# Loads of x and of the first weights asked for in turn, and x transposed and split inside the first product item of a two-block transformer kernel

## What is computed

```
def rmsnorm(x, g):
    xf = x.astype(jnp.float32)
    y = xf * lax.rsqrt(jnp.mean(xf * xf, axis=-1, keepdims=True) + EPS)
    return (y * g.astype(jnp.float32)).astype(x.dtype)
...
        h = rmsnorm(x, g_mix[l])
        z = jnp.einsum('bsd,dc->bsc', h, w_in[l])
        cb, cc, cv, q, k, v, f_logit, gate_c, gate_a = jnp.split(z, SPLIT_POINTS, axis=-1)
```

## Time and profile before

| what | us |
|---|---|
| time, median of 3 runs | 2446.07 |
| lowest and highest of them | 2444.16, 2447.24 |
| the profiled execution's own time | 2443.27 |
| its span in the trace | 2441.5 |

### The profile page before, as it was taken

One profiled execution on the slowest core, in us unless ns is written; L12 is line 12 of the kernel. 1 busy time (PEld: TensorE's weight loads), 2 busy tenths in 40 slices (PEclk: granted clock), 3 DMA queues, 4 the chain that ended last, 5 costly groups with the idle time before them and its releaser, 6 DMA issues.

```text
span 2441.5 us, 30339 instructions
## 1 busy us (share of the span) xinstructions
PE 2418.8 (99%) x12645; PEld 2060.3 (84%) x12645; DVE 1515.2 (62%) x1534; ACT 1168.7 (48%) x1360; POOL 0.2 (0%) x4
## 2 busy tenths in 40 slices
PE   8999999999999999999999999999999999999999
PEld 6788888888888888888888888888888888888887
DVE  5565566666566556566456666855777577756774
ACT  5444444545544344344344545554555455535552
POOL 0000000000000000000000000000000000000000
PEclk9999999999999999999999999999999999999999
DMA  7546556565555565655665555545656665566564
GB/s 227 175 151 192 158 183 188 183 189 189 189 178 189 195 216 184 195 177 198 195 185 177 198 153 172 172 170 179 189 175 206 190 189 174 200 195 181 183 203 143
DMA packets 236902, 450.58 MB, mean 185 GB/s; under 512 B 16449, under 2 KB 19643, under 8 KB 236635
## 3 DMA queue, kind: packets, MB, share of 16 engines
q1 hardware_dynamic: 235995, 447.49, 57.8%
q10 hardware_dynamic: 768, 1.14, 0.1%
HBM read 446.46 MB, written 2.11 MB: 184 GB/s over the span
## 4 chain that ended last, share of the span: by engine, by line
PE 96%; DVE 2%; ACT 1%; DMA 0%; issue 0%; SPq 0%; DVEq 0%; ACTq 0%
PE PS L69 96%; DVE WL L69 1%; ACT WH L69 1%; DVE TA L69 0%; DMA RAW<-in_w_in 0%; DVE TC L69 0%; DVE XT L69 0%; DVE TB L69 0%; ACT TA L69 0%; DVE PB L69 0%; DVE NC L69 0%; DVE XHL L69 0%; SPq L69 0%; DVE DG L69 0%; DVE K L69 0%
## 5 line engine op out<-in xcount | busy, mean ns | idle before, releaser
L69 DVE TENSOR_TENSOR WL<-RAW,WH 128x1024 fp32r<-128x1024 f32 (+1 forms) x844 | 1022.0, 1220 | 780.8 <-ACT WH L69 780.6
L69 PE MATMUL PS<-XHL,WH 128*128 128x512 f32 x3984 | 1406.6, 399 | 6.6 <-DVE XHL L69 5.9
L69 ACT ACTIVATE WH<-RAW 128x1024 fp32r<-128x1024 f32 (+1 forms) x845 | 881.6, 1054 | 940.7 <-PE PS L69 924.5
L69 PE MATMUL PS<-XHL,WL 128*128 128x256 f32 x3968 | 1112.8, 280 | 0.0
L69 PEld LDWEIGHTS PS<-XHL,WH 128*128 128x128 f32 x3984 | 748.2, 188 | 192.3 <-DVE XHL L69 6.1
L69 PEld LDWEIGHTS PS<-XHL,WL 128*128 128x128 f32 x3968 | 750.3, 189 | 0.5
L69 PE MATMUL PS<-WH,MHL 128*128 128x512 f32 x2240 | 694.8, 390 | 1.0 <-DVE TA L69 1.0
L69 PEld LDWEIGHTS PS<-WH,MHL 128*128 128x128 f32 x2240 | 420.5, 188 | 88.8 <-DVE TA L69 1.4
L69 PE MATMUL PS<-WL,MHL 128*128 128x512 f32 x1120 | 435.8, 389 | 0.0
L69 PEld LDWEIGHTS PS<-WL,MHL 128*128 128x128 f32 x1120 | 210.3, 188 | 42.9
L69 DVE TENSOR_TENSOR TA<-TA,PS 128x1024 f32<-128x1024 f32 x72 | 87.9, 1221 | 7.9 <-ACT TA L69 0.5
(11 more groups left out here) (126 smaller groups left out, 821.5 us busy)
## 6 DMA issues: line engine op xcount, KB each, us to landing
RAW<-in_w_ff SPq DMA_DIRECT2D x256, 512.0 KB, 3.7
RAW<-in_w_in SPq DMA_DIRECT2D x224, 512.0 KB, 3.8
RAW<-in_w_up SPq DMA_DIRECT2D x176, 512.0 KB, 3.9
RAW<-in_w_down SPq DMA_DIRECT2D x88, 512.0 KB, 4.2
RAW<-in_w_mix_out SPq DMA_DIRECT2D x32, 512.0 KB, 4.1
RAW<-in_w_out SPq DMA_DIRECT2D x32, 512.0 KB, 3.6
RAW<-in_w_conv_out SPq DMA_DIRECT2D x16, 512.0 KB, 3.6
RAW<-in_w_attn_out SPq DMA_DIRECT2D x16, 512.0 KB, 4.2
```

Of the source, the lines that this page charges most:

```text
L69: ins = step[1](*step[2], **step[3])
```

## The change

The loads are asked for in another order: piece 0 of x, unit 0, piece 1, unit 1, and so on to piece 4 and unit 4. The transposes of x go into banks 4 to 7 only, each used twice. Pairs 0 and 1 are transposed and split in front of the first item; pair n + 2 is transposed and split behind unit n of the first item (n = 0 to 5), through `mid`. The first item takes banks 0 to 3 at once. The squares become pending behind unit 5 and no longer in front of unit 0; `norm_columns` is called behind unit 6 and no longer behind unit 4; `spread_item` stays behind unit 7. The transpose of the gain (`PS<-CONST,VR`) comes ahead of pair 0.

```
         for i, (c0, c1) in enumerate(((0, 256), (256, 512), (512, 1024), (1024, 1536), (1536, 2048))):
             SP.dma(nc.sync.dma_start, XT[:, :, c0:c1], xd[:, :, c0:c1], s_x[i])
-        load_to(NR - 1)
+            load_to(i)
         SP.dma(nc.sync.dma_start, CONST[:, P:C_N], io["const"][:, P:C_N], s_const)
...
-        pend = []
-        PE.wait([(s_id, 16)])
-        for u in range(8):
-            if u == 1:
-                PE.wait([(s_gm, 16)])
-                t = PE.do(nc.tensor.transpose, PS[:, 7, 0:16], VR[0:16, 0, :], ID[0:16, 0:16])
-                gm_t = V.do(nc.vector.tensor_copy, VEC[:, 0:16], PS[:, 7, 0:16], after=[t])
-            PE.wait([(s_x[x_piece[u]], 16), gm_t if u == 7 else None])
+        def turn_first(u):
+
+            bank = 4 + u % 4
+            PE.wait([(s_x[x_piece[u]], 16), turned.get(u - 4)])
             for c in range(2):
                 for tb in range(2):
-                    e = PE.do(nc.tensor.transpose, PS[:, u, c * T + tb * P:c * T + (tb + 1) * P],
+                    e = PE.do(nc.tensor.transpose, PS[:, bank, c * T + tb * P:c * T + (tb + 1) * P],
                               XT[:, tb, (2 * u + c) * P:(2 * u + c + 1) * P], ID, inc=c == 1 and tb == 1)
-            pend.append(e)
+            if u:
+                split_to(u)
+            turned[u] = split_bank(XHL, 2 * u, PS[:, bank, :], G_MIX + 2 * u, [e, gm_t], xtok)
+            if u == 7:
+                free[1] = [turned[u]]
+
+        turned = {}
+        free[1] = None
+        PE.wait([(s_id, 16), (s_gm, 16)])
+        t = PE.do(nc.tensor.transpose, PS[:, 7, 0:16], VR[0:16, 0, :], ID[0:16, 0:16])
+        gm_t = turned[-1] = V.do(nc.vector.tensor_copy, VEC[:, 0:16], PS[:, 7, 0:16], after=[t])
         first = wide(w1, 0, ALLK, C0["q"])
-        for u in range(8):
-            v = split_bank(XHL, 2 * u, PS[:, u, :], G_MIX + 2 * u, [pend[u], gm_t], xtok)
-            free[u // 4] = [v]
-            if u < NS:
-                split_to(u)
+        split_to(0)
+        turn_first(0)
+        turn_first(1)
...
-        later(first_squares())
...
-        it = feature_item(first, XHL, xtok, {4: [lambda: norm_columns("r1", "sum")], 7: [lambda: spread_item("r1")]})
+        mid = {n: [lambda u=n + 2: turn_first(u)] for n in range(6)}
+        mid[5].append(lambda: later(first_squares()))
+        mid[6] = [lambda: norm_columns("r1", "sum")]
+        mid[7] = [lambda: spread_item("r1")]
+        it = feature_item(first, XHL, xtok, mid)
```

## The result

| kernel | median, us | lowest to highest | runs |
|---|---|---|---|
| before | 2444.59 | 2443.49 to 2447.24 | 16 |
| changed | 2449.98 | 2447.98 to 2453.18 | 16 |

The ratio of the changed kernel to the one before is 1.0022, with a 95% interval of 1.0015 to 1.0029: 5.4 us slower (3.7 to 7.1), where 6.75 had been forecast. In absolute figures the forecast of 2452.8 lies 2.8 us above the measured median; 1.48 of that is only that the three runs of before, from which it started, had a higher median (2446.07) than the 16 here. The profiled execution of the changed kernel took 2449.13 us with a span of 2447.3, which is 5.8 more than the span of before.

The account below looks back on a forecast made before the run. PE, busy 99% of the span, was taken as the bound, so start delays reach the end: stall 4.25 plus clock terms 0.6, 0.9 and 1.0 gave 6.75 us slower, 2446.07 + 6.75 = 2452.8; range 2449.2 to 2456.0.

Parts of the forecast that it names:

- The mechanism: First item: unit 2 waits for unit 4's load, and decisively the spread waits for the late norm; second item 4.25 us later.
- The rest: PE idle ahead of the spread, from 40.0 until the diagonals stand at 46.7: 6.8 us, with the clock certain to fall.
- the slow spread: The spread after PE's rest, run at the low clock: 1.19 us and not 0.61, so 0.6 more.
- the 1.0 for the clock at unit 2: A 3.4 us rest before unit 2 drops the clock; unit 2 lasts 4.1 to 4.5 us, costing 0.8 to 1.2.
- The chain from the last turning of x to the diagonals: Pair 7's high halves, splits of units 10 and 11, eight squares and norm steps, from 34.5 to 46.7: 12.2 us.
- The curve by amounts: Early loads land in the order asked for, 1.37 us per 512 KB, each placed at its amount on the earlier trace's curve.
- the signs: What the changed trace should show, including PE gaps before unit 2 and the spread, and the second item 5 to 6 us later.
- The 0.83 for four: Time on PE for four transposes of x in the first item, about 0.21 us each.
- The clock behind the spread: Clock back 3.2 to 4.1 us after the restart, so the second item loses 0.7 to 1.1 us, taken as 0.9.
- rival 4: Both clock losses at their worst, clock back only 5 to 6 us after each restart: up to 2.5 more, 2455.3; chance 0.05.
- second item later, without clock: First matmul of the second item at 47.95 against 43.70, from the stall at the spread: 4.25 us.
- Rival 3: Norm chain fits PE's 5.5 us left in units 6 and 7, no stall at the spread: 2443.6 or 2439.7; chance 0.08.

Follow-up runs that it names:

- the kernel with turning ahead of splits: Changed kernel with pairs 2 to 6 turned and split ahead of the splits of the following units, squares still late: 2447.42 us, ratio 1.0012.
- the first with the filled rest: Changed kernel with 28 unread 512-column matmuls issued ahead of the wait for the diagonals, first of two sets of runs: 2450.65 us, ratio 1.0017.
- the one with the norm sooner: Changed kernel, pairs 2 to 7 turned ahead of following splits, squares two at a time behind pairs 3 to 6, norm behind unit 4: 2442.27 us, ratio 0.9988.
- the kernel with both waits away: Changed kernel, pairs 2 to 6 turned ahead of following splits, squares two at a time behind pairs 3 to 6, norm behind unit 5: 2443.00 us, ratio 0.9992.

## Why the prediction was right, and which terms were off

**The mechanism stood.** Removing the late squares turns a loss of 6.16 us at the mark into a gain of 3.05, and putting them late in the kernel before costs 10.1 alone. The rest was forecast as 6.8 us and measured as 6.82. The second item was forecast at 48.55 (47.95 and 0.6 for the slow spread), or 49.55 with the 1.0 for the clock at unit 2, and came at 47.88. The chain from the last turning of x to the diagonals took 12.4 us (33.67 to 46.09) where 12.2 had been added up. The total owes something to luck, since two terms of about 1 us each were wrong in opposite directions.

**The loads.** The curve by amounts held: ACT, which waited for the loads, began the split of unit 0 at 5.95 (landing forecast for 6.3), of unit 4 at 16.35 (16.9) and of unit 5 at 20.94 (21.0). Unit 2 started at 19.20 (19.6), unit 3 at 23.70 (23.7).

**Unit 0 and the first rest: a term that comes and goes.** The prediction read the granted clock of 1.00 before 15.7 us as full speed, and let unit 0 run 2.77 us. It ran 5.3 (8.80 to the transposes at 14.06), at 0.64 us a pair: PE was at the low clock from the beginning. So unit 1 ended later, the rest at unit 2 was 0.99 and not 3.4 us, and the clock did not fall there: in this trace the term "1.0 for the clock at unit 2" was zero. In the second trace of the same kernel unit 0 ran 4.66, the rest was 2.00, and the clock did fall; the wait for unit 5's load took most of the loss, and 0.4 us of it reached the spread. So that term is real in some executions, its forecast size was too large in both traces, and its sign, a gap of about 3 us with the clock at 0.5 behind it, was fully seen in neither. Nor did the second item start 5 to 6 us later, as the signs had it, but 4.18 and 4.58.

**The transposes: mis-sized.** The 0.83 for four came from the earlier trace rows, 24 in 5.18 us, taken to be at full clock. They were at the low one. In the changed kernel four at full clock last 0.60 to the end of the last, and a unit with its turning takes 3.27 (26.59 to 29.86), so 0.5 for four. Three of them at 0.33 less account for pair 7 being turned at 33.7 in place of 34.5, and the second item starts 0.7 earlier than the 48.55.

**The clock behind the spread: mis-sized the other way.** The forecast was 0.9 us, from a return 3.2 to 4.1 us after the restart. It came back 6.2 us after (46.14 to about 52.3), and the loss to the mark is 1.98. The case of a clock back "5 to 6 us after each restart" stood in the prediction as rival 4, and for this restart it was right. It is tempting to blame the broken start, since PE issues the spread, waits 0.52 us for `RB`, and only then goes on. The record speaks against it as the whole cause. With that same break the clock came back 4.7 us after the start of the spread in the kernel with turning ahead of splits, 7.1 in the changed kernel's second trace and 7.4 in the kernel with late squares. And at the norm of the earlier trace rows, where PE rests 2.94 us and goes on without a break, the time was 3.2 us in the kernel before and 5.8 in the changed kernel's second trace:

```profile
1430.22 1.19 PE L69 MATMUL PS<-DG,CONST 128*128 128x128 f32 x4 [2.94 <-DVE DG L69]
```

It was about 6.0 in the kernel before with loads in turn, in the first with the filled rest and in the one with the norm sooner. So the return differs by some 3 us between executions at one and the same place, and the prediction's 3.2 to 4.1, taken from two restarts of one trace, was too narrow. What decides it stays open.

| term, us | forecast | measured in the trace |
|---|---|---|
| second item later, without clock | 4.25 | 3.57 (4.18 - 0.61) |
| spread at the low clock | 0.6 | 0.61 |
| low clock behind the spread | 0.9 | 1.98 |
| low clock at unit 2 | 1.0 | 0 |
| sum | 6.75 | 6.16 at the mark |

This is the first trace; at the mark of the second the loss was 6.90. Of the 6.16 the two spans keep 5.8 and the medians 5.4. The step from 6.75 to 5.4 is thus in part the errors above and in part the scatter of whole runs (3.7 to 7.1).

**The rule that was set aside.** By the Trainium skill ("TensorE: Matmul & The Clock Gate", the section on the clock gate) a ramp need not be modelled, being below 1% of a span. The runs bear it out in size, 2.6 us here being 0.1%, and show that for a change of 0.2% it is still two fifths of the answer. The same section says that the throttled clock is the default and that activity releases it; the trace agrees, with 0.64 us a pair in unit 0, and the row of the granted clock, which says 1.00 there, does not.

**Rival 3** (faster) was rightly held unlikely for this kernel, and its condition was right: it decides at the length of the norm's chain. With the squares in ACT's gaps the second item started at 40.64 against its 41.2.

## What to carry to other kernels

When a start-up is cut into steps so that the matrix engine can begin sooner, follow the longest side chain that has to end inside the same item, and count it from its new place in each engine's list: here 12 us of splits, squares and norm were left with 5.6 us of cover, and that cost more than the early start gave. Small work on a side engine belongs into stretches where that engine waits for a load anyway, and not behind the last splits. And try each half of a change alone: one moved line, the order of the loads, gave 2.7 us by itself (0.5 to 4.9).

## What the runs showed of the hardware

The granted clock in the profile's rows cannot be trusted at the start of a trace. In the changed kernel the row

```profile
9.00:12.00 3.00, 3.00 (x10) 2.52 (x11) 2.02 (x4) 1.70 (x3) 0.00 (x0) 1.00 1.03 384
```

says 1.00 while PE issues a pair each 0.64 us, the rate of the earlier trace rows at a granted clock of 0.50; full speed is about 0.35 (15.19 to 15.54 in the same trace). In the kernel with loads in turn no stretch up to 66 us shows less than 1.00, and yet its pairs are 0.64 us apart from 16.78 to 20.11. The spacing of equal matmuls is the better clock, and the first units of a kernel should be costed at the low one.

The return of the clock after a rest took 3.2 us (at 1422 us in the kernel before), 4.1 us (at 18.43), and 6.2 us (the changed kernel's spread), and over all the traces here 3.2 to 7.4. Nor does the length of a rest alone say whether the clock falls: it fell at unit 2 in two traces with a rest of 2.00 us, and did not with 2.15 in the first kernel with the filled rest, with 2.42 ahead of the spread in the kernel with both waits away, and with 2.94 in that kernel's later norm:

```profile
1419.82 0.68 PE L69 MATMUL PS<-DG,CONST 128*128 128x128 f32 x4 [2.94 <-DVE DG L69]
```

The spread takes 0.68 us there and 1.19 in the row at 1430.22. The rest of 6.8 us in the changed kernel cost 2.6 us beyond itself (0.61 and 1.98); with the rest filled the mark came 2.3 us sooner, and 2.9 between the second traces.
